# Expert weights laid out with eight successive rows per partition and loaded two units at a time, in a decoder layer with 32 experts

## The chip, the cores and the metric

The kernel runs on one core of a Trainium2 chip. The metric is the device time of one execution in microseconds (us); of several executions the median is given. A core has engines that work side by side, each on its own list of instructions: TensorE (PE in the profile, PEld for its weight loads), VectorE (DVE), ScalarE (ACT), GpSimd (POOL) and SyncE (SP, which here only issues transfers). Sixteen DMA engines move data between HBM and the on-chip memory (SBUF). Engines wait for one another by semaphores.

## What is computed

One decoder layer on 512 tokens of width 1024: a time-mixing and attention stage, and then an expert stage in which each token goes through 4 of 32 experts. What matters here is the expert stage:

```
def expert_block(args):
    tok, gate, e = args
    hid = xt[tok] @ w1[e] + b1[e]
    out = clamped_swiglu(hid) @ w2[e] + b2[e]
    return out * gate[:, None].astype(out.dtype)
...
def clamped_swiglu(h):
    glu, lin = h[..., ::2], h[..., 1::2]
    ...
    return glu * jax.nn.sigmoid(SWIGLU_ALPHA * glu) * (lin + 1.0)
```

`w1[e]` is 1024 x 2048 and `w2[e]` 1024 x 1024, both float32, so an expert has 12 MB of weights and all 32 have 384 MB. Both products sum over 1024 rows of the weight matrix. A sum may take its rows in any order, if the activations are put in the same order.

## The kernel before

The stages ahead of the experts are written out in a fixed order for each engine, and the change touches one of their products. The expert stage begins at about 448 us of the span. It goes through the 32 experts one after the other, in **blocks** of up to NS = 96 tokens (further blocks for experts with more tokens follow where there are any; here there are none).

An expert's weights are cut into UNITS = 12 **units** of 1 MB: eight of w1 (`w1_unit`, one for each group of 128 rows) and four of w2 (`w2_unit`, one for each 256 rows). A unit lies in SBUF as 128 partitions x 8192 bytes. Twelve units have room, in a ring: unit number n goes to `raw[n % 12]`. Two neighbours of the ring lie side by side in one region of the tensor `slots`. TensorE works through the units in order; a w1 unit and a w2 unit are each three groups of 32 tokens times four column parts. After each unit it raises `unit_used`.

SyncE issues the loads in the order of use: for each expert the eight units of its w1, then the four of the w2 of the expert before it (`next_units`). Ahead of a load it waits in `wait_used` until TensorE has used the unit that lay in the place (number n - 12), and the load raises a semaphore of its place, `raw_loaded`, for which TensorE waits in `wait_loaded`.

```
def load_w1(eng, e, k, n):
    eng.dma_start(raw[n % RAW].rearrange("p (k c) f -> p k (c f)", k=1),
                  W1_T[:, bass.ds(e, 1), k:k + 1, :].rearrange("p a k f -> p (a k) f"))\
       .then_inc(raw_loaded[n % RAW], 16)
```

At the start of the stage the ring fills in steps. SyncE issues six units of expert 0 early, four of expert 1 ahead of the last row store (L707), and then, once the rows are stored in HBM, the last two of expert 0 and the following ones as places come free.

TensorE alternates: the eight w1 units of block b, then the four w2 units of block b - 1. Beside it:

- GpSimd gathers the 96 token rows of a block from `h2_rows` in HBM into `xg` (L943, for expert 1 L924), and adds the finished rows of a block to `x_sum` in HBM by an indirect transfer (L955). Both are queued apart from SyncE's loads, on the same 16 DMA engines.
- VectorE turns the gathered rows, so that the 1024 features lie along the partitions (`turn_x`, 12 transposes of 32 x 256, L2185). After w1 it adds the bias (L2228, which frees TensorE's banks), forms the activation (L2232 to L2236) and turns that (`turn_act`, 16 transposes of 32 x 192, L2195); w2 of the block waits for this by `a_ready`.
- The rows of expert 0 aren't gathered. TensorE picks and turns them by a product with 0/1 matrices (`first_tokens`, L1493), whose stationary operand is a 128 x 128 piece of `h2row`.

Of the kernel before, what the change touches and what calls it, by code (L numbers as in the profile page):

```python
# [6 lines left out]
def hymba_layer(nc, x, attn_norm_g, w_in, mu, w0, w_up, a0, a_up, g_up, k_k, k_a, r_k, ln_w, ln_b,  # L7
# [11 lines left out]
    P = 128  # L19
# [13 lines left out]
    NS = 96  # L33
# [32 lines left out]
    with ctx:  # L66
# [128 lines left out]
        raw = [slots[:, RING[r // 2], r % 2 * 4:r % 2 * 4 + 4, :] for r in range(RAW)]  # L195
# [211 lines left out]
        raw_loaded = [sem(f"raw_loaded{r}") for r in range(RAW)]  # L407
# [176 lines left out]
        def wait_loaded(eng, i, n):  # L584

            eng.wait_ge(raw_loaded[n % RAW], i * (2 * UNITS // RAW * 16) + (n // RAW + 1) * 16)
# [7 lines left out]
        W1_T = w1[0].rearrange("e (k p) f -> p e k f", p=P)  # L594
        W2_T = w2[0].rearrange("e (j p h) f -> p e j (h f)", p=P, h=2)

        def load_w1(eng, e, k, n):
            eng.dma_start(raw[n % RAW].rearrange("p (k c) f -> p k (c f)", k=1),  # L598
                          W1_T[:, bass.ds(e, 1), k:k + 1, :].rearrange("p a k f -> p (a k) f"))\
               .then_inc(raw_loaded[n % RAW], 16)  # L600

        def load_w2(eng, e, j, n):
            eng.dma_start(raw[n % RAW].rearrange("p (k c) f -> p k (c f)", k=1),  # L603
                          W2_T[:, bass.ds(e, 1), j:j + 1, :].rearrange("p a k f -> p (a k) f"))\
               .then_inc(raw_loaded[n % RAW], 16)
# [5 lines left out]
        def _(sp):  # L611
# [82 lines left out]
            for r in range(FIRST):  # L694
                sp.sem_inc(raw_loaded[r], 16)
            for k in range(W1U - 2):
                load_w1(sp, 0, k, FIRST + k)
            for tt in range(TT):
                for half in range(2):
                    emptied(sp, "o", tt, half)  # L700
                if tt < TT - 1:
                    sp.wait_ge(hrow_ready, TT + tt + 1)
                else:
                    for u in range(FIRST):
# [6 lines left out]
            for k in range(W1U - 2, W1U):  # L711
                load_w1(sp, 0, k, FIRST + k)

            def next_units(i, q, e, e_before, begun=0):
                for u in range(begun, UNITS):
                    n = q * UNITS + u
                    wait_used(sp, i, n - RAW)
# [11 lines left out]
            for j in range(W2U):  # L729
                wait_used(sp, E // 2, j - RAW)  # L730
                load_w2(sp, E - 1, j, j)
            sp.wait_ge(tables_ready, 1)
            npairs = sp.value_load(pairs_i[0:1, 0:1], min_val=E // 2, max_val=NB // 2)
            with sp.Fori(E // 2, NB // 2) as i:
                with sp.If(i < npairs):
                    for q in range(2):
                        e = sp.value_load(blkexp[0:1, bass.ds(i * 2 + (q - E), 1)], min_val=0, max_val=E - 1)
                        for u in range(UNITS):
                            n = W2U + q * UNITS + u
                            wait_used(sp, i, n - RAW)  # L740
# [540 lines left out]
        def _(pe):  # L1281
# [200 lines left out]
            def first_tokens(tt):  # L1482
# [9 lines left out]
                for k in range(KT):  # L1492
                    ins = nc.tensor.matmul(bank[6 + k // 4][:, (k % 4) * NS:(k % 4 + 1) * NS], h2row[:, tt, k * P:(k + 1) * P],  # L1493
# [297 lines left out]
        def _(dve):  # L1791
# [570 lines left out]
```

## Time and profile before

| | |
|---|---|
| median of 3 runs | 1537.73 us (1536.8 to 1537.91) |
| the profiled execution, its own time | 1541.62 us |
| its span, first to last instruction | 1539.9 us |
| TensorE busy with matmuls | 1437.1 us (93%) |
| VectorE busy | 963.8 us (63%) |
| weight loads of the expert stage | 384 of 1024 KB each |
| chain that ended last | PE 40%, DMA 33%, DVE 12%, SP's queue 10% of the span |
| mean granted TensorE clock | 0.983 of full speed |

The chain is followed backwards from the last instruction, at each step to what released it. "PE" busy is the time in which matmuls are under way. A share of the DMA engines near 1 says that all 16 work all the time; it can pass 1 a little, since packets overlap.

### The profile page before, as it was taken

The page shows a single profiled execution, that of the slowest core. Times are in us where ns is not written, and L with a number is a line of the kernel's source. Part 1 is how long each engine was busy: PE and PEld are TensorE (multiplying, and loading weights), DVE is VectorE, ACT ScalarE, POOL GpSimd, SP SyncE. Part 2 cuts the span into 40 slices and gives each one's busy share as a digit, 9 for nine tenths or more (in the row PEclk, how much of TensorE's full clock was granted, in tenths as well). Part 3 has the DMA queues.
Part 4 walks back from the last instruction along what each step waited for, and adds up shares of the span by engine and source line. Part 5 has one row for each costly group of instructions (what it writes and reads, how often), then busy time and mean ns, then how long its engine had stood idle before and what let it go on. Part 6 is the DMA issues. An engine that isn't in the chain of part 4 may idle for free.

```text
span 1539.9 us, 31449 instructions
## 1 busy us (share of the span) xinstructions
PE 1437.1 (93%) x12450; PEld 627.7 (41%) x12450; DVE 963.8 (63%) x1821; ACT 256.4 (17%) x461; POOL 317.3 (21%) x428
## 2 busy tenths in 40 slices
PE   9999999898999999999999999999999999999992
PEld 7777878786552233332222222222222222222220
DVE  5499856642446977576665566666556666655664
ACT  4535243320310010001000000100000010000012
POOL 5633551331230001111111111111111111111100
PEclk9999989999999999999999999999999999999996
DMA  5422100130559999999999999999999999999984
GB/s 177 167 78 80 37 17 6 56 110 1 203 216 394 392 402 402 397 392 402 395 396 387 399 384 394 400 393 390 390 395 389 394 396 391 388 394 388 393 333 132
DMA packets 96785, 456.24 MB, mean 296 GB/s; under 512 B 22978, under 2 KB 36968, under 8 KB 47567
## 3 DMA queue, kind: packets, MB, share of 16 engines
q1 hardware_dynamic: 86974, 434.49, 71.7%
q0 software_dynamic: 9600, 20.31, 5.3%
q8 instruction: 46, 0.75, 0.2%
q10 hardware_dynamic: 144, 0.52, 0.1%
q14 instruction: 21, 0.16, 0.0%
HBM read 442.89 MB, written 20.61 MB: 301 GB/s over the span
## 4 chain that ended last, share of the span: by engine, by line
PE 40%; DMA 33%; DVE 12%; SPq 10%; issue 3%; ACT 2%; POOL 0%; DVEq 0%; POOLq 0%; ACTq 0%
DMA slots<-in_expert_w_dram 32%; PE banks L1709 15%; PE banks L1718 8%; SPq L598 6%; PE banks L1651 3%; SPq L603 3%; PE banks L1439 1%; PE banks L1324 1%; PE banks L1325 1%; PE banks L1326 1%; DVE AR L1947 1%; PE banks L1425 1%; PE banks L1536 1%; PE banks L1504 1%; PE banks L1412 1%
## 5 line engine op out<-in xcount | busy, mean ns | idle before, releaser
L1709 PE MATMUL banks<-slots,BK 128*32 128x512 f32 x6144 | 673.6, 594 | 22.6 <-DMA slots<-in_expert_w_dram 21.6
L1709 PEld LDWEIGHTS banks<-slots,BK 128*32 128x32 f32 x6144 | 195.9, 110 | 490.7 <-issue 368.8
L2228 DVE TENSOR_TENSOR qk<-banks,qk 128x1536 f32<-128x1536 f32 x32 | 56.3, 1758 | 276.2 <-PE banks L1709 275.9
L955 POOL DMA_INDIRECT x_sum<-hT,idy x32 | 46.6, 1457 | 675.7 <-issue 577.0
L1718 PE MATMUL banks<-slots,qk 128*32 128x512 f32 x1536 | 172.5, 594 | 13.2 <-DMA slots<-in_expert_w_dram 13.2
L1718 PE MATMUL banks<-slots,hT 128*32 128x512 f32 x1536 | 171.6, 593 | 13.7 <-DMA slots<-in_expert_w_dram 13.0
L2185 DVE STREAM_TRANSPOSE BK<-AR 32x256 f32<-32x256 f32 x384 | 167.0, 435 | 18.8 <-DMA AR<-h_rows,idx 12.8
L1243 ACT ACTIVATE BK<-qk 128x768 f32<-128x768 f32 x32 | 30.5, 952 | 676.9 <-DVE qk L2228 676.9
L1718 PEld LDWEIGHTS banks<-slots,qk 128*32 128x32 f32 x1536 | 47.7, 109 | 135.1 <-issue 93.6
L1718 PEld LDWEIGHTS banks<-slots,hT 128*32 128x32 f32 x1536 | 47.6, 109 | 134.9 <-issue 93.1
L2195 DVE STREAM_TRANSPOSE qk<-AR 32x192 f32<-32x192 f32 x256 | 94.7, 370 | 3.8
L2195 DVE STREAM_TRANSPOSE hT<-AR 32x192 f32<-32x192 f32 x256 | 94.7, 370 | 3.8
L784 POOL TENSOR_TENSOR u_lo<-slots,u_hi 128x1024 fp32r<-128x1024 f32 x26 | 63.8, 2454 | 86.0 <-ACT u_hi L1036 85.9
L1324 PE MATMUL banks<-h_hi,u_lo 128*128 128x512 f32 x200 | 79.1, 396 | 2.5 <-POOL u_lo L784 1.3
L2213 DVE SCALAR_TENSOR_TENSOR hT<-banks,shiftbuf,lnw 32x512 f32<-32x512 f32 x64 | 47.4, 740 | 52.0 <-ACT lnw L1238 51.4
L1326 PE MATMUL banks<-h_hi,u_hi 128*128 128x512 f32 x200 | 77.9, 390 | 0.0
L1325 PE MATMUL banks<-h_lo,u_hi 128*128 128x512 f32 x200 | 77.8, 389 | 0.0
L1238 ACT ACTIVATE lnw<-banks,shiftbuf 64x512 f32<-64x512 f32 x32 | 21.9, 684 | 272.6 <-PE banks L1718 272.6
L1651 PE MATMUL banks<-slots,hT 128*128 128x512 f32 x128 | 57.0, 597 | 0.0
L2213 DVE SCALAR_TENSOR_TENSOR hT<-banks,shiftbuf,stepm 32x512 f32<-32x512 f32 x64 | 47.6, 744 | 0.9
L2213 DVE SCALAR_TENSOR_TENSOR hT<-banks,shiftbuf,lnb 32x512 f32<-32x512 f32 x64 | 47.5, 742 | 0.9
L1324 PEld LDWEIGHTS banks<-h_hi,u_lo 128*128 128x128 f32 x200 | 37.5, 188 | 12.5 <-ACT shiftbuf L1075 2.0
(380 smaller groups left out, 1446.0 us busy)
## 6 DMA issues: line engine op xcount, KB each, us to landing
slots<-in_expert_w_dram SPq DMA_DIRECT2D x384, 1024.0 KB
slots<-in_w_in_dram SPq DMA_DIRECT2D x13, 1024.0 KB, 5.2
xs<-in_x_dram SPq DMA_DIRECT2D x8, 512.0 KB, 5.1
slots<-in_w_out_dram SPq DMA_DIRECT2D x2, 2048.0 KB, 8.7
x_sum<-slots POOLq DMA_DIRECT2D x1, 2560.0 KB
h_rows<-slots SPq DMA_DIRECT2D x4, 512.0 KB, 7.9
slots<-x_sum SPq DMA_DIRECT2D x4, 512.0 KB, 4.8
out_dram<-hT SPq DMA_DIRECT2D x3, 512.0 KB, 2.6
```

The source lines that it names most:

```text
L598: eng.dma_start(raw[n % RAW].rearrange("p (k c) f -> p k (c f)", k=1), W1_T[:, bass.ds(e, 1), k:k + 1, :].rearrange("p a k f -> p (a k) f"))\
L784: nc.gpsimd.tensor_tensor(u_lo[n % 2][:, :, :], w_in_raw[n // 2 % 2][:, :, n % 2 * P:(n % 2 + 1) * P], u_hi[n % 2][:, :, :], ALU.subtract) ...
L1324: nc.tensor.matmul(out, w_l(k), h_hi[:, k, :], start=(k == 0), stop=False)
L1325: nc.tensor.matmul(out, w_h(k), h_lo[:, k, :], start=False, stop=False)
L1326: ins = nc.tensor.matmul(out, w_h(k), h_hi[:, k, :], start=False, stop=(k == KT - 1))
L1651: ins = nc.tensor.matmul(ps[:, :], hT[:, k, tt * P:(tt + 1) * P], slots[:, st[2], k, :], start=(k == 0), stop=(k == KT - 1))
L1709: ins = nc.tensor.matmul(bank[HID + g][j * CB:(j + 1) * CB, :], xT[q][:, k, g * CB:(g + 1) * CB], raw[n % RAW][:, j, :], start=(k == 0), s ...
L1718: ins = nc.tensor.matmul(bank[first_bank + g][c * CB:(c + 1) * CB, :], actT[q][:, c // 2 * 4 + j, g * CB:(g + 1) * CB], raw[n % RAW][:, c, ...
L2185: ins = nc.vector.transpose(xT[q][a * CB:(a + 1) * CB, :, g * CB:(g + 1) * CB], rows[:, a])
L2195: ins = nc.vector.transpose(at[a * CB:(a + 1) * CB, j], rows[:, a])
L2213: ins = nc.vector.scalar_tensor_tensor(ob[g * CB:(g + 1) * CB, q, half * CW:(half + 1) * CW], bank[first_bank + g][at, :], gates_at[at, g, ...
L2228: tensor_tensor(inner, hid, bias_row.unsqueeze(1).to_broadcast([P, NG, CW]), ALU.add).then_inc(hid_free, 1)
```

## The change

The same 12 MB are loaded and the same products are made, with these edits:

- The rows of w1 and w2 are dealt out in another way: partition p now holds rows 8p to 8p + 7. Unit k of w1 was the rows 128k to 128k + 127; it is now rows k, 8 + k, 16 + k and so on. So two successive units are two successive rows of w1 (four of w2) in each partition, 16384 bytes in one piece in HBM. From one partition to the next the address steps by 64 KB in w1 and 32 KB in w2; before, a unit was 1 MB in one piece.
- A load brings two units, 2 MB in 128 runs of 16384 bytes. There are six semaphores `raw_loaded` in place of twelve, one for each pair. SyncE waits until both units of a pair are used, and TensorE's wait for either unit of a pair is met when the whole pair has landed.
- The activations follow the new order: `turn_x` and `turn_act` read with a step of eight elements (`turn_act` stepped by two before), the picked piece of `h2row` in `first_tokens` steps by eight (it was contiguous), and w2 takes another piece of `actT`.
- `turn_act` is one transpose over 128 partitions in place of 16 over 32 partitions. `turn_x` still has 12.

```diff
-        raw = [slots[:, RING[r // 2], r % 2 * 4:r % 2 * 4 + 4, :] for r in range(RAW)]
+        pair_of = [slots[:, r] for r in RING]
+        raw = [pair_of[r // 2][:, r % 2 * 4:r % 2 * 4 + 4, :] for r in range(RAW)]
...
-            eng.wait_ge(raw_loaded[n % RAW], i * (2 * UNITS // RAW * 16) + (n // RAW + 1) * 16)
+            eng.wait_ge(raw_loaded[n % RAW // 2], i * (2 * UNITS // RAW * 16) + (n // RAW + 1) * 16)
...
-        W1_T = w1[0].rearrange("e (k p) f -> p e k f", p=P)
-        W2_T = w2[0].rearrange("e (j p h) f -> p e j (h f)", p=P, h=2)
+        W1_P = w1[0].rearrange("e (p k) f -> p e k f", p=P)
+        W2_P = w2[0].rearrange("e (p k) f -> p e k f", p=P)
...
-            eng.dma_start(raw[n % RAW].rearrange("p (k c) f -> p k (c f)", k=1),
-                          W1_T[:, bass.ds(e, 1), k:k + 1, :].rearrange("p a k f -> p (a k) f"))\
-               .then_inc(raw_loaded[n % RAW], 16)
+            eng.dma_start(pair_of[n % RAW // 2].rearrange("p k f -> p (k f)"),
+                          W1_P[:, bass.ds(e, 1), k:k + 2, :].rearrange("p a k f -> p (a k f)"))\
+               .then_inc(raw_loaded[n % RAW // 2], 16)
...
-                for u in range(begun, UNITS):
+                for u in range(begun, UNITS, 2):
                     n = q * UNITS + u
-                    wait_used(sp, i, n - RAW)
+                    wait_used(sp, i, n + 1 - RAW)
...
-                    ins = nc.tensor.matmul(bank[6 + k // 4][:, (k % 4) * NS:(k % 4 + 1) * NS], h2row[:, tt, k * P:(k + 1) * P],
+                    ins = nc.tensor.matmul(bank[6 + k // 4][:, (k % 4) * NS:(k % 4 + 1) * NS], h2row[:, tt, k::KT],
...
-                                               actT[q][:, c // 2 * 4 + j, g * CB:(g + 1) * CB],
+                                               actT[q][:, 2 * j + c // 2, g * CB:(g + 1) * CB],
...
-                    rows = xg[g * CB:(g + 1) * CB, q, :].rearrange("p (k a f) -> p a k f", a=4, f=CB)
+                    rows = xg[g * CB:(g + 1) * CB, q, :].rearrange("p (a f k) -> p a k f", a=4, k=KT)
...
-                at = actT[q].rearrange("p (h j) (g s) -> p j g h s", h=2, g=NG)
-                for j in range(4):
-                    rows = act[j * CB:(j + 1) * CB].rearrange("p g (a f h) -> p a g h f", a=4, h=2)
-                    for a in range(4):
-                        ins = nc.vector.transpose(at[a * CB:(a + 1) * CB, j], rows[:, a])
-                ins.then_inc(a_ready, 1)
+                nc.vector.transpose(actT[q].rearrange("p m (g s) -> p g m s", g=NG),
+                                    act.rearrange("p g (f m) -> p g m f", m=KT)).then_inc(a_ready, 1)
```

The instructions issued by SyncE in the loop over the experts stand as follows before, from the last w2 load of one block to the w1 units 0 to 3 of the next (ISA and REGISTER_ALU are the waits and address sums ahead of a load, L608 loads the bias):

```order
L603 DMA slots<-in_expert_w_dram 128x2048
L590 REGISTER_ALU
L598 ISA
L598 DMA slots<-in_expert_w_dram 128x2048
L590 REGISTER_ALU
L598 ISA
L598 DMA slots<-in_expert_w_dram 128x2048
L590 REGISTER_ALU
L608 ISA
L608 DMA qk<-in_expert_b_dram 4x512
L598 ISA
L598 DMA slots<-in_expert_w_dram 128x2048
```

And in the changed kernel, at the same place (its lines are one or so further on):

```order
L604 DMA slots<-in_expert_w_dram 128x4096
L591 REGISTER_ALU
L599 ISA
L599 DMA slots<-in_expert_w_dram 128x4096
L591 REGISTER_ALU
L609 ISA
L609 DMA qk<-in_expert_b_dram 4x512
L599 ISA
L599 DMA slots<-in_expert_w_dram 128x4096
```

One load with one wait stands where two loads with two waits stood; the bias load keeps its place, behind units 0 and 1.

On VectorE, from the transposes of the gathered rows to those of the activation, one block before reads:

```order
L2185 STREAM_TRANSPOSE BK<-AR 32x8x32 x12
L2202 STREAM_SHUFFLE qk<-qk 128x512
L2203 REGISTER_ALU
L2204 TENSOR_SCALAR qk<-qk 128x256
L590 ISA
L2228 TENSOR_TENSOR qk<-banks,qk 128x1536
L2232 TENSOR_SCALAR shiftbuf<-qk 128x768
L2234 TENSOR_TENSOR AR<-qk,BK 128x768
L2235 ISA
L2236 SCALAR_TENSOR_TENSOR AR<-AR,shiftbuf 128x768
L2195 STREAM_TRANSPOSE qk<-AR 32x3x2x32 x16
```

In the changed kernel the last of these rows differs, and the row ahead of it stands as before:

```order
L2233 SCALAR_TENSOR_TENSOR AR<-AR,shiftbuf 128x768
L2192 STREAM_TRANSPOSE qk<-AR 128x3x8x32
```

Nothing has moved on VectorE; the sixteen instructions have become one.

## Rows read from the trace of the kernel before

**Rows 1.** Page, section 2, forty slices of the span.

```profile
PE   9999999898999999999999999999999999999992
...
DMA  5422100130559999999999999999999999999984
```

**Rows 2.** Waits of TensorE: us in total, times, longest us.

```profile
PE banks L1718 <- DMA slots<-in_expert_w_dram: 26.2, 40, 1.4
PE banks L1709 <- DMA slots<-in_expert_w_dram: 21.6, 23, 1.0
```

**Rows 3.** Windows: length, busy us of each engine, granted clock, DMA share, GB/s.

```profile
454.00:1486.00 1032.00, 980.17 (x8957) 283.96 (x8949) 660.48 (x1319) 86.24 (x123) 129.63 (x213) 1.00 1.01 393
...
908.00:912.00 4.00, 4.00 (x40) 0.97 (x32) 0.60 (x2) 0.00 (x0) 0.00 (x0) 1.00 1.05 331
```

**Rows 4.** Chain that ended last, 900 to 1000 us: start, us, what.

```profile
892.97 28.84 DMA slots<-in_expert_w_dram
```

**Rows 5.** Transfers: count, size of each, median us to landing.

```profile
slots<-in_expert_w_dram SPq DMA_DIRECT2D x384, 1024.0 KB
...
slots<-in_w_out_dram SPq DMA_DIRECT2D x2, 2048.0 KB, 8.7
```

**Rows 6.** Windows with one kind of transfer: expert weights, then output projection's.

```profile
408.00:412.00 4.00, 4.00 (x17) 2.27 (x16) 3.69 (x15) 1.62 (x3) 0.96 (x1) 1.00 1.01 426
311.00:312.00 1.00, 1.00 (x14) 0.93 (x10) 0.63 (x1) 0.47 (x2) 1.00 (x2) 1.00 1.02 395
```

**Rows 7.** SyncE's queue at the start of the expert stage.

```profile
453.90 4.69 SPq L598 DMA_DIRECT2D slots<-in_expert_w_dram  x6
461.93 6.93 SPq L603 DMA_DIRECT2D slots<-in_expert_w_dram  x4
478.35 2.90 SPq L598 DMA_DIRECT2D slots<-in_expert_w_dram  x2
```

**Rows 8.** Chain at the start of the expert stage.

```profile
454.77 8.62 DMA AR<-h_rows,idx
463.41 0.43 DVE BK L2185
...
472.89 12.97 PE banks L1709 x96
485.85 0.66 PE banks L1700 x2
486.51 2.71 PE banks L1709 x24
```

**Rows 9.** Windows at the start of the expert stage.

```profile
456.00:478.00 22.00, 18.68 (x151) 6.13 (x144) 12.38 (x24) 2.65 (x3) 7.46 (x10) 0.84 1.01 403
478.00:486.00 8.00, 8.00 (x77) 2.21 (x70) 5.74 (x16) 0.00 (x0) 0.00 (x0) 1.00 1.01 317
```

**Rows 10.** TensorE at the end of the expert stage.

```profile
1483.41 5.38 PE L1709 MATMUL banks<-slots,BK 128*32 128x512 f32 x48 [0.61 <-DMA slots<-in_expert_w_dram]
1488.61 10.48 PE L1718 MATMUL banks<-slots,qk 128*32 128x512 f32 x96
1499.82 10.51 PE L1718 MATMUL banks<-slots,hT 128*32 128x512 f32 x96 [0.72 <-DVE hT L2195]
```

**Rows 11.** Groups of VectorE: count, busy us, mean ns, idle us before.

```profile
L2185 DVE STREAM_TRANSPOSE BK<-AR 32x256 f32<-32x256 f32 x384 | 167.0, 435 | 18.8 <-DMA AR<-h_rows,idx 12.8 <-DVE pairs_i L2276 0.2
L2195 DVE STREAM_TRANSPOSE hT<-AR 32x192 f32<-32x192 f32 x256 | 94.7, 370 | 3.8
L2228 DVE TENSOR_TENSOR qk<-banks,qk 128x1536 f32<-128x1536 f32 x32 | 56.3, 1758 | 276.2 <-PE banks L1709 275.9
```

**Rows 12.** Reductions of 128 elements: contiguous (L2031), then step 32 (L2037).

```profile
L2031 DVE TENSOR_REDUCE slotf<-BK x4: 286/286/289, 409.4 to 448.2; 128x4 f32<-128x128 f32 x4
...
L2037 DVE TENSOR_REDUCE all_gates<-BK x4: 374/374/384, 410.4 to 450.0; 128x32 f32<-128x128 f32 x4
```

**Rows 13.** Weight loads of the picking product of the first block.

```profile
L1493 PEld LDWEIGHTS banks<-shiftbuf,slots x64: 187/192/193, 436.1 to 447.0; 128*128 128x128 f32 x64
```

More of the change, by code:

```diff
@@ L406, in hymba_layer @@
         xg_loaded = [sem(f"xg_loaded{q}") for q in range(2)]
-        raw_loaded = [sem(f"raw_loaded{r}") for r in range(RAW)]
+        raw_loaded = [sem(f"raw_loaded{r}") for r in range(RAW // 2)]
         g2_in = sem("g2_in")
@@ L592, in hymba_layer @@
         block = ctx.enter_context(nc.Block())
-        W1_T = w1[0].rearrange("e (k p) f -> p e k f", p=P)
-        W2_T = w2[0].rearrange("e (j p h) f -> p e j (h f)", p=P, h=2)
+        W1_P = w1[0].rearrange("e (p k) f -> p e k f", p=P)
+        W2_P = w2[0].rearrange("e (p k) f -> p e k f", p=P)
         def load_w1(eng, e, k, n):
-            eng.dma_start(raw[n % RAW].rearrange("p (k c) f -> p k (c f)", k=1),
-                          W1_T[:, bass.ds(e, 1), k:k + 1, :].rearrange("p a k f -> p (a k) f"))\
-               .then_inc(raw_loaded[n % RAW], 16)
+            eng.dma_start(pair_of[n % RAW // 2].rearrange("p k f -> p (k f)"),
+                          W1_P[:, bass.ds(e, 1), k:k + 2, :].rearrange("p a k f -> p (a k f)"))\
+               .then_inc(raw_loaded[n % RAW // 2], 16)
         def load_w2(eng, e, j, n):
-            eng.dma_start(raw[n % RAW].rearrange("p (k c) f -> p k (c f)", k=1),
-                          W2_T[:, bass.ds(e, 1), j:j + 1, :].rearrange("p a k f -> p (a k) f"))\
-               .then_inc(raw_loaded[n % RAW], 16)
+            eng.dma_start(pair_of[n % RAW // 2].rearrange("p k f -> p (k f)"),
+                          W2_P[:, bass.ds(e, 1), 2 * j:2 * j + 4, :].rearrange("p a k f -> p (a k f)"))\
+               .then_inc(raw_loaded[n % RAW // 2], 16)
         def load_bias(eng, e, q):
@@ L693, in _ @@
             emptied(sp, "Y", TT - 1)
-            for r in range(FIRST):
+            for r in range(FIRST // 2):
                 sp.sem_inc(raw_loaded[r], 16)
-            for k in range(W1U - 2):
+            for k in range(0, W1U - 2, 2):
                 load_w1(sp, 0, k, FIRST + k)
@@ L703, in _ @@
                 else:
-                    for u in range(FIRST):
+                    for u in range(0, FIRST, 2):
                         load_w1(sp, 1, u, UNITS + u)
@@ L710, in _ @@
             sp.wait_ge(xt_full, 2)
-            for k in range(W1U - 2, W1U):
+            for k in range(W1U - 2, W1U, 2):
                 load_w1(sp, 0, k, FIRST + k)
             def next_units(i, q, e, e_before, begun=0):
-                for u in range(begun, UNITS):
+                for u in range(begun, UNITS, 2):
                     n = q * UNITS + u
-                    wait_used(sp, i, n - RAW)
+                    wait_used(sp, i, n + 1 - RAW)
                     if u == 2:
@@ L728, in _ @@
                     next_units(i, q, i * 2 + q, i * 2 + (q - 1))
-            for j in range(W2U):
-                wait_used(sp, E // 2, j - RAW)
+            for j in range(0, W2U, 2):
+                wait_used(sp, E // 2, j + 1 - RAW)
                 load_w2(sp, E - 1, j, j)
@@ L737, in _ @@
                         e = sp.value_load(blkexp[0:1, bass.ds(i * 2 + (q - E), 1)], min_val=0, max_val=E - 1)
-                        for u in range(UNITS):
+                        for u in range(0, UNITS, 2):
                             n = W2U + q * UNITS + u
-                            wait_used(sp, i, n - RAW)
+                            wait_used(sp, i, n + 1 - RAW)
                             if u == 2:
```

## The prediction

> **What bounds the kernel now.** I read the forty slices first. From the thirteenth slice on both TensorE and the DMA engines show nine tenths or more [rows 1], so the expert stage, two thirds of the span, is close to two limits at once. Which of them ends last is told by TensorE's waits: it waits for expert weights 26.2 us in w2 and 21.6 us in w1, in 63 pieces of at most 1.4 us, 47.8 us together [rows 2]. The windows say the same: from 454 to 1486 us the DMA share is 1.01, while TensorE is busy 980.17 of 1032 us [rows 3]. The chain shows how far the transfers are behind: a unit lands 28.84 us after its issue, and TensorE, which has waited for it, takes it up at once [rows 4]. In 28.84 us eleven units go by at the stage's rate of 1032/366 = 2.82 us (384 units less 10 loaded ahead of 454 us and 8 behind 1486), so nearly the whole ring of twelve is on its way and TensorE uses what has just landed. **The transfers bound this stage**, and TensorE is 5% behind them: nothing that shortens VectorE's work alone can shorten the stage, and the transfers can gain at most some 48 us before TensorE takes over.
>
> The rate isn't even. Weights alone come at 426 GB/s with a share of 1.01 [rows 6]; from 908 to 912 us it is 331 at 1.05 [rows 3]: there the indirect transfers of the tokens share the engines.
>
> **Term 1, the length of a run.** The 384 loads of 1024 KB [rows 5] consist of 128 runs of 8192 bytes, 49152 in all, 3072 for each of 16 engines. They become 1536 runs of 16384 bytes per engine. What a run costs beyond its bytes can be read from two stretches with one kind of transfer. Weights alone move at 426 GB/s with a share of 1.01, which is 421.8 for a share of 1; the output projection (L683, runs of 2048 bytes) moves at 395 with 1.02, which is 387.3 [rows 6]. On one of 16 engines a run of 8192 bytes then takes 16 x 8192 / 421.8 = 310.7 ns and one of 2048 takes 84.6 ns. The line through both has 36.8 ns for each 1000 bytes and **9.2 ns for each run**. With 16384 bytes a run takes 612.2 ns instead of twice 310.7, and 1536 x 9.2 ns = 14.1 us are saved per engine; for the 366 units of the stage 13.5 us. A share of 1.00 in place of 1.01 would shift either rate by 1%, so the 9.2 ns are known to about 5 either way: 6 to 21 us. The load's closing packets halve too, which I can't price from a row and leave inside these bounds. I take **-13.5**.
>
> The token transfers keep their number of packets; each waits behind a longer run of weights, which delays them and doesn't move more bytes. A gather takes 8.62 us to land at the start [rows 8]. It has 96 rows, six for each engine; if each stands behind one run, it becomes 6 x 0.30 = 1.8 us later. Within the loop this is covered: VectorE waits 275.9 us in 32 blocks ahead of L2228 for TensorE, 8.6 us in each block [rows 11].
>
> **Term 2, waiting for pairs.** In the steady part the DMA engines always have some ten units in front of them, so a load that is issued one unit later (2.62 us, a quarter of the 10.48 of w2 [rows 10]) starts no later. This fails where the ring isn't yet behind: at the start. There 10 units are issued from 453.90 to 468.9 us, and the next only at 478.35, when TensorE frees it [rows 7]. From 456 to 478 the engines move 22 x 403 = 8.87 MB, 8.5 units with the few token rows in it [rows 9]. So at 478.35 only 1.4 units are left, about 4.3 us at the 317 GB/s of those microseconds [rows 9]: until 482.7. In the changed kernel the first pair of expert 2 is issued when its second unit is used, near 481.0, and its data begin to flow some 2 us later: 483 us at the best. (The output projection's 2 MB land 8.7 us after their issue [rows 5], of which 5.4 are the bytes at 387.3 GB/s; of the 3.3 left I give 2 to the time ahead of the first byte.) The cover is used up. The next pairs follow TensorE: four units take 12.97 us up to 485.9, and from there each unit 2.71 behind a product of 0.66 [rows 8], so the second unit of a pair is done at 485.9, 492.6 and 499.3 us, and those of w2 at 504.6 and 509.9. With 2 us to the first byte and 5.0 us for a pair at 420 GB/s the engines stand still for 0.3, 0, 0.9, 1.7, 0.3 and 0.3 us, **3.5** in all.
>
> What comes ahead of this may move it too. At the start the gather, twelve transposes and the bias addition stand on the chain to TensorE [rows 8], so the gather's 1.8 us come on top there. The transposes now read with a step of eight elements. The nearest rows are two reductions of 128 elements: 286 ns where they are read in a row and 374 with a step of 32 [rows 12], 0.69 ns per element more at most (more elements are written as well). For a transpose of 256 elements that is 0 to 177 ns on 435 [rows 11], for twelve 0 to 2.1 us. Of these 0 to 4 us I take 1.5, near the gather's part, since that one has a cause in the packets. Together **+5**, bounds 0 and 9.
>
> **Term 3, the tail.** TensorE takes up the last two w1 units at 1483.41, the first as soon as it has landed, and waits once more for the other inside this stretch [rows 10]. Now both start when the second has landed: one unit, **+2.6**. Behind it w2 of the block before covers VectorE's chain for 10.48 us, and 0.72 us of it stick out [rows 10]. That chain ends in `turn_act`.
>
> **Term 4, `turn_act`.** Sixteen transposes of 370 ns [rows 11] are 5.9 us for a block. A transpose of 192 elements takes 370 and one of 256 takes 435 ns, 1.02 ns per element and 175 fixed. One instruction of 768 elements is then 0.96 us; with the 0.69 ns for a step, 1.5 us. The bounds are 0.96 and 5.9, if the engine took the four groups of partitions in turn. So 4.4 us of VectorE's work go in each block, 141 us in all, and nearly nothing of it shows: the next reader is w2 of the block, eight w1 units (21 us) later. At the very end it removes the 0.72 us: **-0.7**.
>
> On SBUF lines the trace and a page go together only in sign. The reduction that steps by 32 elements is 88 ns longer [rows 12]. The Trainium skill ("SBUF — State Buffer", Door 1: The DMA port swizzle) says that lines are 16 bytes and that each access that crosses to a new line pays, so that four float32 is how far one can step for free. By it all the steps of eight pay, the step of two before didn't; what it costs it doesn't say, and the sum above holds without it.
>
> **Term 5, the picking product.** Its 64 weight loads take 192 ns each [rows 13] and now read with a step of eight. No row shows a weight load with a step. If a load took the 0.69 ns for each of 128 columns, it would be 88 ns and 5.6 us for all, of which the last two groups of sixteen stand ahead of the first unit: 2.8 us, and 12 if it doubled for all. Nothing is gained by it. TensorE loads 128 values of float32 in 192 ns, slowly enough for SBUF; I take **0**. The cover is SyncE's own wait until 453.90 [rows 7], for 6 us.
>
> **Sum.** -13.5 + 5 + 2.6 - 0.7 + 0 = **-6.6 us**. It is made against the profiled execution, 1541.62 us by its own time, 1539.9 of span: 1535.0. The median of the runs is 1537.73, 3.9 us lower than that execution; on it the sum gives **1531 us**, 0.4% less.
>
> **The rivals.**
>
> *Nothing gained per run, waits added (slower).* If the 9.2 ns belong to the shape of the output projection's load and not to a run, term 1 is 0 and 5 + 2.6 - 0.7 = +7 remain: 1545 us. For it: two windows, one of them 1 us long, carry the term. Against: it decides only if term 1 is below 4 us, less than its own error allows. The same sign comes from the addresses. Before, sixteen engines read within 1 MB at a time; now their runs lie 64 KB apart from one partition to the next. If that costs 3% of the stage's 1032 us, it is +31 and 24 in the sum, 1562 us; it turns the sign from 0.7% on. No row here has such a step, so the trace leaves it open.
>
> The Trainium skill ("DMA: Bandwidth & Descriptors", Latency and other measured facts) speaks against the change here: rows of 16 KiB whose pitch is 512 KiB were copied at 207 GB/s where 214 is full, and at 164 with 2 MiB. Its smallest loss, 3%, is at eight times the pitch of w1; by the trend the loss at 64 KB is nearly none.
>
> *The slow stretches get better (much faster).* From 908 to 912 us the rate is 331 [rows 3] where weights alone have 426 [rows 6]. If part of the loss comes with each change between weights and token rows, half as many weight runs may halve it: two stretches of some 4 us per block with a fifth lost make 1.7 us per block, half of it 0.8, for 31 blocks 26 us. With the sum that is -33: 1505 us. It can't go on past the 47.8 us of waits [rows 2]. Against: the number of token rows is the same, and it may be they that cost.
>
> *The start doesn't wait.* If the gaps of term 2 stay shut and the run's cost is at its upper bound: -21 + 2.6 - 0.7 = -19, 1519 us.
>
> *The change shows nothing.* Terms 1 and 2 cancel within 3 us of either side.
>
> **How the numbers follow.** Chances: the forecast with its neighbours from -12 to -3 us 0.33; shut start or dearer runs (-12 to -20) 0.15; better slow stretches 0.09; within 3 us (0.2% of 1537.73, about what a measurement can tell) 0.18; slower by term 1 failing 0.13; slower by the addresses 0.12. That makes 0.57 faster, 0.18 same, 0.25 slower. The range from 1514 to 1548 takes in the bounds of terms 1 and 2 and the first half of the slow rival, and leaves out the large cases, 0.09 and about 0.1.
>
> **What would show it.** The packets of the weights' queue should fall by 24576. The share stays near 1.01 from 480 to 1480 us, and a window with weights alone should show 428 GB/s at a share of 1, not 422. TensorE's waits for weights should fall from 47.8 to some 35 us, in longer pieces. At 478 to 515 us the share should drop below 1 in places. `turn_act` should be 32 instructions of 1 to 1.5 us; `turn_x` 435 to 610 ns. The forecast is wrong if the rate with weights alone is below 422 (addresses), if the windows around 331 GB/s rise (the fast rival), or if weight loads of the picking product pass 280 ns.

## The result and the profile after

The changed kernel takes **1546.92 us** in the median of 7 runs (1543.01 to 1551.98), the kernel before 1537.74 in 7 runs (1536.8 to 1538.79). The ratio is 1.0058, with a 95% interval from 1.0045 to 1.0071: **9 us or 0.6% slower**, where 6.6 us faster was forecast. The time lies within the range; its sign was the other one. The profiled execution took 1546.92 us by its own time, with a span of 1545.2, so the two profiles differ by 5.3 us and the medians by 9.2. The rest is on the other side: the kernel before took 1541.62 in its profiled execution and 1541.78 in that of a second profile, 3.9 and 3.7 above the medians (1537.74 and 1538.09), and the changed kernel's equals its median. Why, I don't know.

The weights' queue in the page's table of queues (packets, MB, share of the 16 engines' span):

```profile
q1 hardware_dynamic: 59326, 434.47, 71.3%
```

Before, the same line had 86974 packets and 71.7%. The share times the span is the time that an engine spends on this queue: 1104.1 us before and 1101.7 now, so 2.4 us less where term 1 alone had said 14 (the share has one decimal, so either time is good to 0.8 us). The packets fall by 27648: the 24576 that were forecast, and 16 more for each of the 192 loads that are gone. Weights alone and the steady part, in windows (columns as in [rows 3]):

```profile
408.00:412.00 4.00, 4.00 (x11) 1.81 (x10) 1.19 (x2) 0.99 (x2) 3.06 (x3) 1.00 1.04 446
406.00:414.00 8.00, 8.00 (x26) 3.93 (x25) 2.98 (x10) 1.62 (x3) 4.03 (x4) 1.00 1.01 426
560.00:1480.00 920.00, 870.82 (x7988) 255.33 (x7984) 523.46 (x715) 78.43 (x112) 112.69 (x189) 1.00 1.00 394
```

446 / 1.04 is 429 GB/s for a share of 1, against 422 in [rows 6]; 428 was forecast. This isn't a confirmation: the window has only four microseconds, single ones of which read from 410 to 475, and the 8 us around it give 426 / 1.01 = 422, as before. The steady part is no faster: TensorE's busy time in 560 to 1480 us tells roughly how far it gets, and it is 870.82 us here, 872.80 in the first profile of the kernel before and 873.96 in its second.

TensorE's waits for weights, which answer to [rows 2]:

```profile
PE banks L1710 <- DMA slots<-in_expert_w_dram: 34.7, 41, 1.8
PE banks L1719 <- DMA slots<-in_expert_w_dram: 14.4, 20, 1.6
```

49.1 us against 47.8, in w1 more than in w2 now. The timeline of TensorE at the start of the stage:

```profile
439.37 4.10 PE L1494 MATMUL banks<-shiftbuf,slots 128*128 128x96 f32 x16
...
448.62 4.09 PE L1494 MATMUL banks<-shiftbuf,slots 128*128 128x96 f32 x16
452.65 21.78 PE L1710 MATMUL banks<-slots,BK 128*32 128x512 f32 x192
476.32 0.64 PE L1691 MATMUL banks<-ident,all_gates 128*96 128x128 f32 x4 [1.89 <-DVE qk L2225]
...
514.33 7.93 PE L1710 MATMUL banks<-slots,BK 128*32 128x512 f32 x72 [3.14 <-DVE qk L2225]
```

A group of sixteen picking matmuls (L1494, before L1493) takes 4.1 us; the first w1 unit starts at 452.65 us. In the profile before these were 2.0 us and 447.68. But the stage ahead had ended earlier in this profile: the first group begins at 433.53 us, before at 436.53. From there to the first w1 unit are 19.1 us against 11.2, so TensorE reaches it 8.0 us later, and all four groups count. At 514.33 TensorE has waited 3.14 us for VectorE, before 0.70 at 510.35. The causes stand in the groups of weight loads and of VectorE, which answer to [rows 13] and [rows 11]:

```profile
L1494 PEld LDWEIGHTS banks<-shiftbuf,slots x64: 312/336/338, 433.1 to 452.1; 128*128 128x128 f32 x64
```

```profile
L2186 DVE STREAM_TRANSPOSE BK<-AR 32x256 f32<-32x256 f32 x384 | 246.2, 641 | 9.3 <-DMA AR<-h_rows,idx 3.4
```

And from the transfers, the token rows (last number: us from issue to landing):

```profile
AR<-h_rows,idx POOLq DMA_INDIRECT x32, 10.9
```

A stepped weight load takes 336 ns and not 192, above the 280 that the prediction had named as a sign of being wrong. A transpose of `turn_x` takes 641 and not 435, and `turn_act` is 32 instructions of 1.58 us in the mean. TensorE's granted clock fell as well, which no term had. The same window before and then after:

```profile
441.00:454.00 13.00, 12.48 (x122) 8.24 (x124) 5.77 (x28) 2.14 (x5) 3.87 (x4) 1.00 0.78 302
441.00:454.00 13.00, 13.00 (x67) 11.87 (x70) 4.81 (x22) 1.11 (x4) 3.63 (x5) 0.50 0.61 213
```

That is, the granted clock is 1.00 before and 0.50 after, the lower of the two levels (1.2 of 2.4 GHz), behind a stretch in which TensorE was busy all the time but made few matmuls. It isn't the cause of the slow loads: in the first group, from 433 to 437 us, the clock is 1.00 and the loads take 335 ns in the median. It makes the eight small products between the groups 0.56 us longer (1.33 against 0.77) and the first eight w1 units 0.97 (21.78 against 20.81). The kernel before pays in another place: there TensorE stands for 3.31 us ahead of expert 1, the clock is 0.50 from 472 to 478 us, and the next four w1 units take 13.04 us instead of 10.51.

A gather lands in 10.9 us; it was 8.7 before, so 2.2 later where 1.8 was worked out. Behind the wait at 514 us the transfers run dry for lack of freed places:

```profile
518.00:522.00 4.00, 4.00 (x40) 1.04 (x32) 3.94 (x6) 0.00 (x0) 0.00 (x0) 1.00 0.35 94
```

The DMA share is 0.35 there, and 0.82 at 498 to 502 us.

### The profile page after: what moved, and what is told of

Read it like the earlier page. It is cut to its first block, busy times and chain, and to the rows that moved or that the text cites. A ratio compares the mean times of both kernels' runs of the same rounds, so it can differ in the third digit from the quotient of the medians.

```text
span 1545.2 us, 30235 instructions
## 1 busy us (share of the span) xinstructions
PE 1441.8 (93%) x12450; PEld 637.3 (41%) x12450; DVE 903.0 (58%) x1341; ACT 256.9 (17%) x461; POOL 317.3 (21%) x428
## 3 DMA queue, kind: packets, MB, share of 16 engines
q0 software_dynamic: 9600, 20.31, 5.2%
## 4 chain that ended last, share of the span: by engine, by line
PE 43%; DMA 42%; DVE 11%; issue 2%; ACT 1%; SPq 0%; DVEq 0%; POOLq 0%; POOL 0%; ACTq 0%
DMA slots<-in_expert_w_dram 42%; PE banks L1710 20%; PE banks L1719 5%; PE banks L1652 3%; PE banks L1494 1%; PE banks L1440 1%; PE banks L1325 1%; PE banks L1326 1%; PE banks L1327 1%; PE banks L1505 1%; DVE AR L1948 1%; PE banks L1426 1%; PE banks L1537 1%; PE banks L1413 1%; PE banks L1591 1%
## 5 line engine op out<-in xcount | busy, mean ns | idle before, releaser
L2186 DVE STREAM_TRANSPOSE BK<-AR 32x256 f32<-32x256 f32 x384 | 246.2, 641 | 9.3 <-DMA AR<-h_rows,idx 3.4
L975 POOL COPY idx_all<-ovf_pair 96x2 int32 x28 | 5.2, 186 | 243.6 <-DMA ovf_pair<-slot_tokens,ovf_col 243.6
L1327 PEld LDWEIGHTS banks<-h_hi,u_hi 128*128 128x128 f32 x200 | 37.5, 188 | 8.0
```

Of the source, the lines that this page charges most:

```text
L1327: ins = nc.tensor.matmul(out, w_h(k), h_hi[:, k, :], start=False, stop=(k == KT - 1))
L2186: ins = nc.vector.transpose(xT[q][a * CB:(a + 1) * CB, :, g * CB:(g + 1) * CB], rows[:, a])
```

## The experiments

**Theory A** after the result: the steps of eight, in the picking product and in `turn_x`, cost at the start, where TensorE stands on the path, and the pairs cost what was forecast. **Theory B**: the steady part loses, by the addresses or by the pairs. Each ratio below is to the kernel before on the same chip, with its 95% interval.

### The picking product in a row again

```diff
+        W1_K = w1[0].rearrange("e (k p) f -> p e k f", p=P)
...
-                load_w1(sp, 0, k, FIRST + k)
+                load_first(sp, k, FIRST + k)
...
-                    ... h2row[:, tt, k::KT],
+                    ... h2row[:, tt, k * P:(k + 1) * P],
```

> The changed kernel, but expert 0's w1 is loaded in the old order of rows (two runs of 8192 bytes per partition), so that the picking product reads h2row in a row again; all else as changed. Theory A (the step of eight in the picking product's weight loads shifts the start of the experts by 5 us): its 16 matmuls per group fall from 4.1 back to 1.9 us, the first w1 unit starts near 448 instead of 452.7, and the time falls by 4 to 6 us from 1546.9, to about 1542. Theory B (addresses, or pairs of units, cost it in the steady part): the start moves as well, but the time stays within 2 us of the changed kernel's, since the transfers end last.

1544.7 us, ratio 1.0045 (1.0031 to 1.0059). The product is back at 2.0 us per group and the first w1 unit starts at 444.41. Of this little arrives:

```profile
472.48 1.09 PE L1697 MATMUL banks<-ident,all_gates 128*96 128x128 f32 x4 [6.20 <-DVE qk L2231]
```

TensorE now waits 6.20 us for VectorE on expert 1, where it waited 1.89: the gather and `turn_x` were running in the shadow of the slow product. The restart on expert 1 comes 38.8 us behind the first picking group, where it came 42.8 behind it, so 4.0 earlier. In the time it is about 2 us by the medians, less than the 4 to 6 of theory A and at the bound that theory B had set; the intervals overlap, so this step alone isn't separated from nothing.

### turn_x in a row again, alone

```diff
-                    rows = xg[...].rearrange("p (a f k) -> p a k f", a=4, k=KT)
+                    rows = xg[...].rearrange("p (k a f) -> p a k f", a=4, f=CB)
```

> The changed kernel, and only turn_x reads in a row as before the change (rows of experts 1 to 31 then meet other rows of w1, the work is the same). If the two steps add up at the start: 3 us less than the changed kernel, about 1544. If the picking product's delay hides turn_x (the gather lands in its shadow): under 1.5 us less.

1544.66 us, ratio 1.0040 (1.0025 to 1.0055); by the ratios 2.8 us less than the changed kernel, again with intervals that overlap. About 3 us had been expected if the two steps add up. The restart on expert 1 stays where it was (476.43 us, VectorE's addition there waits for TensorE and not for `turn_x`). The gain is at the third expert:

```profile
512.00 7.93 PE L1710 MATMUL banks<-slots,BK 128*32 128x512 f32 x72 [0.70 <-DVE qk L2225]
```

The wait of 3.14 us is 0.70 again, and TensorE stands 2.3 us earlier at the same unit.

### Both steps gone

Both edits together.

> As the run before, and turn_x also reads in a row as it did before the change; the rows of experts 1 to 31 then meet other rows of w1 than they should, so the values differ, the work doesn't. Theory A with the transposes in it (turn_x at 641 ns instead of 435 delays TensorE near 476 and 512 us, 2.5 us each): 2 to 4 us less than the run before. Theory B: no change against the run before, since VectorE waits for TensorE in every later block.

1541.44 us, ratio **1.0017** (1.0007 to 1.0027). This is clear of the changed kernel's interval: the two steps cost 0.41% or 6.3 us together, more than 2.0 and 2.8, though by less than the errors of the three. That each hid part of the other is seen in the profiles: with the picking product in a row, `turn_x` is on the path to expert 1, whose restart comes 34.8 us behind the first picking group here and 38.8 with `turn_x` stepped; with the picking product stepped, `turn_x` didn't move it. The median is 3.3 us below that with the picking product alone in a row, within the 2 to 4 expected. The first part of theory A holds. It leaves 0.17%, for pairs, longer runs and the short `turn_act` together.

### Pairs alone

The kernel before, with this and the matching waits:

```diff
-            eng.dma_start(raw[n % RAW].rearrange("p (k c) f -> p k (c f)", k=1),
-                          W1_T[:, bass.ds(e, 1), k:k + 1, :] ...
+            eng.dma_start(pair_of[n % RAW // 2].rearrange("p (k c) f -> p k (c f)", k=2),
+                          W1_T[:, bass.ds(e, 1), k:k + 2, :] ...
```

> The kernel before with only the loads changed: two units by one transfer, as two runs of 8192 bytes for each partition, and the waits for pairs; rows, steps and transposes as before. Theory A with terms 2 and 3 as predicted: +5 to +8 us against 1537.7, by gaps of the DMA engines up to 515 us and by one unit at the tail. Rival: a pair costs nothing because the engines are always behind: within 1.5 us of before.

1547.25 us, ratio 1.0050 (1.0032 to 1.0069): +7.7 us. The sum of terms 2 and 3 was 7.6, but it isn't where they said. The start is that of the kernel before: TensorE is at its third expert (the row below) at 509.06 us, with DMA shares from 0.89 up, so gaps of about 1 us. The loss is in the steady part:

```profile
q1 hardware_dynamic: 83902, 434.47, 71.9%
```

```profile
509.06 7.93 PE L1710 MATMUL banks<-slots,BK 128*32 128x512 f32 x72 [0.71 <-DVE qk L2229]
```

```profile
560.00:1480.00 920.00, 862.27 (x7948) 254.15 (x7944) 578.98 (x1135) 78.47 (x112) 112.48 (x189) 1.00 1.01 393
```

71.9% of a span of 1546.8 us are 1112.2 us per engine on the weights, 8.1 more than before, for the same runs of 8192 bytes at a DMA share of 1.01. In 920 us TensorE gets 10.5 us less done than before. So the engines weren't idle, they took longer for the same runs. A gather still lands in 8.7 us, as before: its 2.2 us come with the longer runs, not with the pairs.

Term 3, the tail, can be read here and above. With pairs alone TensorE waits 1.03 us for the last pair of w1 units, where before it waited 0.61 for the first of these two [rows 10]. In the changed kernel it waits for none of the last eight:

```profile
1474.30 20.78 PE L1710 MATMUL banks<-slots,BK 128*32 128x512 f32 x192
```

So the 2.6 us of term 3 don't stand where it put them.

### New order, single loads

The changed kernel with the old loads of one unit:

```diff
-            eng.dma_start(pair_of[n % RAW // 2].rearrange("p k f -> p (k f)"),
-                          W1_P[:, bass.ds(e, 1), k:k + 2, :] ...
+            eng.dma_start(raw[n % RAW].rearrange("p c f -> p (c f)"),
+                          W1_P[:, bass.ds(e, 1), k:k + 1, :] ...
```

> The changed kernel with its new order of rows and its transposes, but one unit per load again, in runs of 8192 bytes at a pitch of 64 KB (w1) and 32 KB (w2). If the addresses cost (theory B), its rate with weights alone is below 420 GB/s and it is clearly slower than before, by 10 us or more. If they don't, it differs from before by the start alone (5 us from the picking product, 2 from turn_x, nothing from pairs): 1543 to 1546.

1546.58 us, ratio 1.0052 (1.0032 to 1.0072), 0.6 us above the span that was expected. Its start is late (in this profile, itself 3.2 us above the median, the first w1 unit comes at 457.29 us). This kernel has both steps and neither pairs nor longer runs, so its 8 us (5 to 11) are a second measure of the steps. The steady part is as good as any:

```profile
560.00:1480.00 920.00, 876.17 (x8048) 253.04 (x8041) 529.64 (x726) 77.91 (x112) 115.35 (x193) 1.00 1.01 395
```

876.17 us of work in 920: **the addresses cost nothing** at 64 KB and 32 KB from partition to partition, and single loads don't have the pairs' loss. This holds for runs of 8192 bytes. That is the half of theory B that falls.

### Without token rows

Three kernels in which the gathers and the additions of rows are still issued, but drop all rows except row 0:

```diff
-                        bounds_check=last_row, oob_is_err=False)\
+                        bounds_check=0, oob_is_err=False)\
...
-                        bounds_check=T, oob_is_err=False).then_inc(store_done[q], 16)
+                        bounds_check=0, oob_is_err=False).then_inc(store_done[q], 16)
```

> The kernel before with the token rows dropped in the same way. The transfers have 424 GB/s by themselves, so TensorE becomes the bound: its waits for weights fall from 48 us to below 10, and the time falls by about 35 to 45 us, to some 1497.

> The kernel before with pairs of units per load (two runs of 8192 bytes per partition), again with the token rows dropped. Theory C: within 3 us of the same without pairs, since the extra time of pairs (9 us with token rows) comes from their mixing with the token rows; what stays is one unit at the tail. Rival (waits for pairs at the start and in the loop): 6 to 9 us above it.

> The changed kernel in which all gathered and added token rows but row 0 are dropped by the bound on their indices, in the loop and ahead of it (experts 1 to 31 compute on stale rows, and the sums aren't added; weights, products and instructions stay). Theory C (loads of 2 MB lose more to the token rows than loads of 1 MB): without token rows the packets of 16384 bytes take 612 ns nearly all, the stage becomes TensorE's at 31.8 us per block or the transfers' at about 29.5, and this kernel is not slower than the kernel before without its token rows by more than the start, 6 us. Rival (pairs cost in the steady part by themselves): it stays 5 us or more slower beyond the start.

The kernel before takes 1475.95 us (ratio 0.9600), with pairs 1476.06 (0.9594), the changed kernel 1487.02 (0.9652). The first is 62 us below the kernel before, where 35 to 45 had been expected and the prediction had put the ceiling at the 47.8 us of waits; what makes up the rest isn't shown. Steady part of the first, then of the second:

```profile
560.00:1000.00 440.00, 440.00 (x4104) 133.25 (x4100) 298.92 (x590) 40.28 (x57) 58.32 (x98) 1.00 1.00 408
```

```profile
560.00:1000.00 440.00, 440.00 (x4108) 133.35 (x4104) 298.79 (x588) 40.02 (x57) 58.32 (x98) 1.00 1.00 408
```

TensorE is busy 440 of 440 us in both. Pairs cost nothing here, and their engine time on the weights is 1089.9 us against 1088.8 (73.9% of 1474.8 and of 1473.3). So **without the token rows the 8 us of pairs are gone**, from the time and from the engine time. The comparison of times alone wouldn't show it, since TensorE is the bound here and would hide gaps; the engine time does. But one rival isn't excluded. Without the token rows the transfers aren't behind either: a load lands 7.3 us after its issue and a pair 9.8, where it was 28.4 and 27.7. So the loss of pairs may need a full queue and not the token rows. Against this stands only a short stretch ahead of the experts, with a full queue and no token rows, where pairs move at 426 GB/s with a share of 1.00 (408 to 412 us), as single loads do in [rows 6].

The changed kernel is 11 us slower even so, without any wait for weights, and not within the 6 expected. That is its start: from the first picking group to the third expert it takes 81.4 us against 72.3 of the kernel before, and the first 72 matmuls there another 2.9 at a granted clock of 0.57 (10.78 us instead of 7.93). With the transfers as the bound part of this is absorbed later.

### Steps of two and four

Runs of 16384 bytes and pairs can be had with smaller steps, if a partition holds two successive rows out of each 256 of w1 and four out of each 512 of w2:

```diff
-        W1_P = w1[0].rearrange("e (p k) f -> p e k f", p=P)
-        W2_P = w2[0].rearrange("e (p k) f -> p e k f", p=P)
+        W1_P = w1[0].rearrange("e (j p h) f -> p e j (h f)", p=P, h=2)
+        W2_P = w2[0].rearrange("e (j p h) f -> p e j (h f)", p=P, h=4)
...
-                nc.vector.transpose(actT[q].rearrange("p m (g s) -> p g m s", g=NG), ...
+                for j in range(4):
+                    rows = act[j * CB:(j + 1) * CB].rearrange("p g (a f h) -> p a g h f", a=2, h=4)
+                    for a in range(2):
...
```

> A third order of rows that keeps runs of 16384 bytes and pairs: partition p holds two successive rows of w1 out of each group of 256, and four of w2 out of each group of 512, so the reads step by two elements (turn_x, picking product) or four (turn_act, in eight transposes); neighbouring partitions' runs touch in HBM. If steps up to four elements are free, as the 16-byte line says, the picking product's loads take 192 ns, turn_x 435 ns, and the time is that of the changed kernel with both steps gone, 1540 to 1543. If any step costs: 1543 to 1547. If the address pitch of 64 KB had cost something in the changed kernel: below 1539.

1547.11 us, ratio 1.0053 (1.0035 to 1.0072): outside what was expected. The groups of VectorE, with a step of two in the first line and of four in the second:

```profile
L2187 DVE STREAM_TRANSPOSE BK<-AR 32x256 f32<-32x256 f32 x384 | 167.2, 435 | 21.6 <-DMA AR<-h_rows,idx 15.7 <-DVE pairs_i L2279 0.2
L2198 DVE STREAM_TRANSPOSE hT<-AR 32x384 f32<-32x384 f32 x128 | 114.1, 892 | 2.1
```

A step of two is free (435 ns, and 196 for the weight loads), a step of four isn't: with the 175 ns that term 4 worked out beside 1.02 ns per element, 892 ns are 1.87 ns per element, and the changed kernel's 641 ns with a step of eight are 1.82. So `turn_act` grows to 7.1 us per block here. But that is off the path except for 1.09 us at the end, and the steps at the start are free. Why this kernel isn't at the level of the one with both steps gone, I can't say: it waits 5.1 us for VectorE on expert 1 where that one waited 3.2, and in the steady part it does 870.10 us of work against 872.38. The table at the end of the experiments places it: 3 us are lost up to the third expert and 3 to 5 behind it, in this profile and in that of the next run. What differs there is the order of rows in HBM, with neighbouring partitions' runs touching, and a `turn_act` of eight instructions. So closer addresses don't help, and the longer runs gain nothing over the pairs alone here (1.0053 against 1.0050).

### The last pair halved

The same kernel, with the last pair of w1 units in two transfers and a semaphore of its own for the second.

> The run before, and the last pair of w1 units (expert 31) is loaded as two transfers of one unit each, so that TensorE can begin on the first half. Term 3 says 2.6 us less than the run before. Rival: nothing (under 1 us), if TensorE isn't waiting for just that pair at the end.

1546.2 us, ratio 1.0040 (1.0025 to 1.0055), 0.9 us less by the medians and 2 by the ratios, with overlapping intervals. The rival (under 1 us) stands better: in the profile of the run before TensorE does the last eight w1 units in one stretch of 20.79 us from 1472.53 on, without a wait, so there was nothing for the halves to shorten.

### Only w2 in the new order

```diff
-        W2_T = w2[0].rearrange("e (j p h) f -> p e j (h f)", p=P, h=2)
+        W2_T = w2[0].rearrange("e (p j h) f -> p e j (h f)", p=P, h=2)
```

with the one transpose in `turn_act`, and the rest as before.

> The kernel before, and only w2 in the new order (eight successive rows per partition), still one unit per load in runs of 8192 bytes; w1, turn_x and the picking product as before. turn_act is then one instruction of about 1.6 us in place of sixteen. It leaves out what cost time and keeps what freed VectorE: 0.7 us less than before by the wait at the very end, that is 1537 to 1538, which can't be told from no change. If the two profiles' 5.9 us of turn_act stood on the path anywhere else, it would be faster by 3 us or more.

1537.05 us, ratio 0.9992 (0.9979 to 1.0004). VectorE's work in the steady window falls from 584.41 to 462.69 us, and the time can't be told from no change: VectorE's work in the steady part isn't on the path. The 0.72 us of [rows 10] ahead of the last w2 product are gone, as term 4 said. This is the version to keep if anything is; it isn't shown to be faster.

### The kernel before again

> The kernel before, unchanged, for a second profile of it: its first one took 3.5 us more than its median. Expected: 1538, and from TensorE's restart on expert 1 (471.80 us in the first profile) to the end of the last w2 product 1035 to 1039 us.

1538.09 us, ratio 0.9996. From TensorE's restart at 473.65 us to the end of the last w2 product are 1036.6 us, 1038.5 in the first profile.

The profiles differ by up to 5 us in what comes ahead of the picking product, which the change doesn't touch. The following lengths, in us, leave this out; the first is from the first group of the picking product to TensorE's start on the third expert, the second from there to the end of the last w2 product:

| | start | rest |
|---|---|---|
| before, first and second profile | 73.8, 72.6 | 1000.0, 999.3 |
| only w2 in the new order | 71.6 | 998.3 |
| pairs alone | 74.3 | 1008.0 |
| new order, single loads | 83.3 | 999.0 |
| changed kernel | 80.8 | 1001.5 |
| picking product in a row | 78.2 | 1000.5 |
| `turn_x` in a row | 78.4 | 1000.6 |
| both steps gone | 72.0 | 1002.8 |
| steps of two and four | 75.1 | 1005.6 |
| last pair halved | 74.7 | 1005.4 |

Each row is one profile. Against the two of the kernel before, the steps of eight cost 7 to 11 us, in the start; pairs in runs of 8192 bytes cost 8 to 9 in the rest, and pairs in runs of 16384 bytes with rows eight apart 0.5 to 3.5 there.

## Why the prediction was wrong

The bound was read rightly: the transfers end last, and no shortening of VectorE's work shows. The sum failed in these steps, the first three by most.

- **Term 5, "slowly enough for SBUF; I take 0".** A weight load with a step of eight takes 336 ns and not 192, each group of sixteen matmuls 4.1 us and not 2.0. All four groups stand ahead of the first unit and not the last two, so TensorE reaches it 8.0 us later, where the working had 2.8. No row showed such a load, and I took the lower end of a range from 0 to 12 us on an argument and not on a row, although the reductions of [rows 12] had just shown a step to cost something. The cover named, SyncE's wait until 453.90, held for SyncE; TensorE's own start wasn't covered. VectorE's chain covers a part: without this step alone the restart on expert 1 comes 4.0 us earlier and the time falls by about 2.
- **Term 2, the transposes of `turn_x`.** 641 ns lie above the bound of 612 that the nearest row gave, and I took 1.5 us for all that lies ahead of TensorE's restart. In the changed kernel it delays the third expert, at 514 us, by 2.3, and I had looked at expert 1 alone. There the picking product's delay covers it, and it comes out (4.1 us) when that is gone. With the picking product the steps cost 6.3 us, where 1.5 had been set for both.
- **Terms 1 and 2 together.** Term 2 put the steady part at nothing, since a load that is issued late "starts no later". The engines don't fall idle, but the same runs take longer: 8.1 us more engine time for pairs alone. Term 1 put the gain of the longer runs at 13.5 and measured 2.4 against single loads. Against the pairs alone, 1112.2 us, it looks like what was forecast: the engine time is 1101.7 in the changed kernel and 1099.1 with both steps gone (71.4% of 1539.4), 10.5 and 13.1 us less. But with steps of two and four it is 8.6 less (71.4% of 1545.6), and without token rows only 2.9 (1089.9 to 1087.0), where a fixed cost of 9.2 ns for each run would give 14. So these runs don't show that cost; they show that the longer runs lose less beside the token rows. In time 5.1 us arrive with both steps gone (ratio 1.0050 to 1.0017) and nothing with steps of two and four.
- **Term 3, the tail.** 2.6 us for a wait that isn't there in the changed kernel: it does the last eight w1 units without one. Term 4 was right: the 0.72 us at the end are gone.
- **The granted clock**, which no term had. It falls behind the slow loads and gives 1.5 us to the loss at the start, and the kernel before loses 2.5 us in another place.

So the ledger reads: pairs +7.7 us, longer runs and one `turn_act` -5.1, the two steps +6.3, in all +8.9. Each part is a difference of measured ratios, so the sum closes by construction. Each is clear of its error (some 2 to 3 us). The middle one holds for rows eight apart and not for the steps of two and four. The steps measured without pairs, by the single loads in the new order, are +8.0, within the error of 6.3.

The rival that came nearest was "nothing gained per run, waits added", 1545 us with 0.13. Its time was nearly right, and this was luck: it had 5 us from gaps at the start and 2.6 from the tail, where the runs show 6.3 from the steps and the rest from the steady part. Its first half, that a run costs nothing for itself, isn't refuted. The address rival is refuted by the single loads in the new order. "The slow stretches get better" is refuted too: the steady part moves at 394 GB/s as before. That the measured time lies within the range is no merit of the mechanism either, since the range reached 1548 for rivals that didn't happen.

What stays open is why loads of 2 MB in runs of 8192 bytes lose 8 us to two of 1 MB, and why those in runs of 16384 bytes mostly don't. That the loss goes away with the token rows is shown; whether it needs them or only the full queue that they leave isn't, nor is the mechanism.

## What to carry to other kernels

Where a layout is changed for the sake of transfers, price the reads that must follow it, on every engine, and where no row shows the step, take the middle of the range and not zero. A fixed cost per run that is read from two windows, one of 1 us, is a guess until a kernel shows it, and what a larger load does beside other traffic has to be measured apart from it: one kernel with the grain alone and one with the run length would have shown both. Look at the start of a pipeline for itself; what the steady part hides isn't hidden there.

## What the runs showed of the hardware

- A stepped read of float32 costs nearly nothing with a step of two (435 ns for a transpose of 256 elements, 196 for a weight load), and for a transpose nearly the same with four as with eight (1.87 and 1.82 ns per element against 1.02). A weight load with a step of eight takes 335 ns, at a granted clock of 1.00 and of 0.50 alike. The Trainium skill ("SBUF — State Buffer", Door 1: The DMA port swizzle) puts the limit at four float32, with at least two hits in a line of 16 bytes; a step of four has only one hit in a line, and here it pays in full. A step of two has two hits and is free. So the measurements bear out the two hits and not the four float32.
- The rows of the tokens, whose queue moves 20.31 MB beside the 434 of the weights and 3.83 when they are dropped, cost 62 us of 1538: without them TensorE becomes the bound and never waits for weights. That queue's engine time falls from 81.6 us (5.3% of 1539.9) to 14.7 (1.0% of 1473.3), that of the weights by 15.3.
- One transpose over 128 partitions and 768 elements takes 1.6 us, sixteen over 32 partitions and 192 elements 5.9. By the 175 ns and 1.84 ns for each of 768 elements it is the time of one group of partitions: the four groups work side by side.
- TensorE's granted clock was 0.50 (1.2 of 2.4 GHz) from 441 to 454 us in the changed kernel, and 0.51 and 0.50 with `turn_x` in a row and with single loads, behind the stepped weight loads; in all kernels whose picking product reads in a row or with a step of two it was 1.00 there.
